# Down projection: both weight sums ahead of the first split, and one low part of 2560 columns for two pieces

## What is computed

```python
h = rms_norm(x, ffn_norm[l])
x = x + conv_ffn(h, w_ffn_up[l], ffn_conv_w[l], ffn_conv_b[l], w_ffn_down[l])

def conv_ffn(h, w_up, conv_w, conv_b, w_down):
    ...
    a, b = jnp.split(u, 2, axis=-1)
    return (jax.nn.silu(a) * b) @ w_down
```

## Time and profile before

| what | value |
|---|---|
| median of 3 runs | 1081.53 us (1081.53 to 1081.56) |
| span of the profiled execution, first to last instruction | 1079.9 us |
| TensorE busy | 1075.4 us of the span |
| VectorE busy | 909.8 us, 1374 instructions |
| ScalarE busy | 630.3 us |
| mean granted TensorE clock | 0.999 of full speed |

### The profile page before, as it was taken

How to read it: one execution, slowest core, us unless ns; L and a number is a source line. 1 busy time by engine, 2 the same in 40 slices (tenths; PEclk the granted TensorE clock), 3 DMA queues, 4 the chain that set the end, 5 groups by cost and what they waited for, 6 DMA issues and landing times.

```text
span 1079.9 us, 18178 instructions
## 1 busy us (share of the span) xinstructions
PE 1075.4 (100%) x6549; PEld 930.3 (86%) x6549; DVE 909.8 (84%) x1374; ACT 630.3 (58%) x926; POOL 70.9 (7%) x100
## 2 busy tenths in 40 slices
PE   9999999999999999999999999999999999999998
PEld 9888888888888888888888888888888888888887
DVE  7878988889655678888888888888877899999997
ACT  7677676756544655555555555545555566646663
POOL 4500000000000000000000000000000000000000
PEclk9999999999999999999999999999999999999999
DMA  8654677777787978888887878788887877887882
GB/s 273 184 157 147 201 199 237 183 243 199 229 234 257 267 212 242 228 240 212 252 226 227 244 212 255 220 238 237 252 231 223 239 250 270 284 276 254 287 313 94
DMA packets 185086, 249.08 MB, mean 231 GB/s; under 512 B 9141, under 2 KB 143174, under 8 KB 184774
## 3 DMA queue, kind: packets, MB, share of 16 engines
q1 hardware_dynamic: 170134, 212.30, 61.0%
q0 software_dynamic: 12480, 31.46, 15.1%
q10 hardware_dynamic: 2416, 4.60, 1.2%
HBM read 243.75 MB, written 36.04 MB: 259 GB/s over the span
## 4 chain that ended last, share of the span: by engine, by line
PE 99%; DMA 0%; DVE 0%; issue 0%; DVEq 0%
PE bank L1791 38%; PE bank L1799 20%; PE bank L2186 7%; PE bank L2185 7%; PE bank L2184 7%; PE bank L2037 3%; PE bank L1838 3%; PE bank L2039 3%; PE bank L1840 3%; PE bank L1839 3%; PE bank L2038 3%; PE bank L1759 1%; PE bank L1867 1%; PE bank L2076 0%; DMA xt<-in_x_dram 0%; PE bank L1956 0%
## 5 line engine op out<-in xcount | busy, mean ns | idle before, releaser
L764 ACT CAST w_hi<-raw 128x1024 fp32r<-128x1024 f32 x299 | 312.2, 1049 | 255.2 <-PE bank L1799 121.9
L1173 DVE TENSOR_TENSOR w_lo<-raw,w_hi 128x1024 fp32r<-128x1024 f32 x299 | 364.2, 1223 | 110.4 <-ACT w_hi L764 109.8
L1791 PE MATMUL bank<-hs,w_hi 128*128 128x512 f32 x1792 | 423.0, 391 | 0.0
L1791 PEld LDWEIGHTS bank<-hs,w_hi 128*128 128x128 f32 x1792 | 331.2, 188 | 66.3 <-issue 0.9
L1799 PEld LDWEIGHTS bank<-hs,w_lo 128*128 128x128 f32 x1792 | 224.5, 191 | 5.7 <-issue 0.2
L1799 PE MATMUL bank<-hs,w_lo 128*128 128x256 f32 x1792 | 227.3, 283 | 0.0
L1143 ACT CAST hi_slot<-slot 128x1024 fp32r<-128x1024 f32 (+1 forms) x96 | 111.0, 1187 | 68.1 <-DVE slot L1716 33.3
L1700 DVE TENSOR_TENSOR slot_lo<-slot,hi_slot 128x1024 fp32r<-128x1024 f32 (+1 forms) x96 | 128.7, 1387 | 4.7 <-ACT hi_slot L1143 3.7
L2186 PE MATMUL bank<-hi_slot,gated 128*128 128x512 f32 (+1 forms) x202 | 78.2, 387 | 0.0
L2184 PE MATMUL bank<-hi_slot,gated 128*128 128x512 f32 (+1 forms) x202 | 78.2, 387 | 0.0
L1618 DVE SCALAR_TENSOR_TENSOR C<-U,cols,C 128x256 f32<-128x256 f32 x176 | 73.3, 479 | 0.0
(11 more groups left out here) (247 smaller groups left out, 1176.7 us busy)
## 6 DMA issues: line engine op xcount, KB each, us to landing
raw<-in_w_ffn_up_dram SPq DMA_DIRECT2D x176, 512.0 KB, 4.8
u_sums<-in_w_ffn_down_dram POOLq DMA_DIRECT2D x60, 512.0 KB, 6.9
raw<-in_w_in_dram SPq DMA_DIRECT2D x51, 512.0 KB, 4.6
slot<-in_w_ffn_down_dram SPq DMA_DIRECT2D x36, 512.0 KB, 5.0
raw<-in_w_in_dram SPq DMA_DIRECT2D x66, 256.0 KB, 3.3
raw<-in_w_out_dram SPq DMA_DIRECT2D x32, 512.0 KB, 5.2
slot<-u_sums SPq DMA_DIRECT2D x60, 256.0 KB, 5.5
slot<-in_w_ffn_down_dram SPq DMA_DIRECT2D x30, 256.0 KB, 4.0
```

Source lines behind the costliest of these rows:

```text
L764: act.copy(w_hi[:, i, :], raw[:, i, :]).then_inc(units_hi, 1)
L1173: dve.tensor_tensor(w_lo[:, i, :], raw[:, i, :], w_hi[:, i, :].bitcast(F32), ALU.subtract)\
L1791: m = pe.matmul(banks[b][:, :], w_hi[:, i, c], hs[:, 4 * i + k, :], start=(first and k == 0), stop=(final and k == 3))
```

## The change

Only VectorE's program for S quadruples changes. Both sums now come first, then the low part of a, and then one subtraction of 2560 columns makes the low parts of b and c together. It waits for the high part of c and then counts `units_split` up by two. The diff also brings code for a third sum in DRAM, for the quadruples named in `SECOND_SUM_IN_DRAM`; that tuple is empty, so the branches that test it never act. The DRAM tensor `u_sums` gets room for three sums per quadruple instead of two, which moves the addresses of the two that are used.

```diff
+SECOND_SUM_IN_DRAM = ()
...
-        u_sums = nc.dram_tensor("u_sums", (SEVENS * 2 * P, 2 * GT), F32)
-        u_sums_v = u_sums.ap().rearrange("(n j p) (c m) -> n j p c m", j=2, p=P, m=GT)
+        u_sums = nc.dram_tensor("u_sums", (SEVENS * 3 * P, 2 * GT), F32)
+        u_sums_v = u_sums.ap().rearrange("(n j p) (c m) -> n j p c m", j=3, p=P, m=GT)
...
-                before = raw_piece_before(q, "c")
-                if before is not None:
-                    wait_until_used(dve, before)
-                elif SLOT_OF[q] == 2:
-                    wait_until_used(dve, LAST_OLD)
-                dve.tensor_tensor(t2, t1, b21, ALU.add).then_inc(t2_made, 1)
-                dve.wait_ge(t2_made, s + 1)
+                if second_sum_in_dram(q):
+                    dve.wait_ge(second_sum_loaded[SLOT_OF[q]], second_sums_loaded(q))
+                else:
+                    before = raw_piece_before(q, "c")
+                    if before is not None:
+                        wait_until_used(dve, before)
+                    elif SLOT_OF[q] == 2:
+                        wait_until_used(dve, LAST_OLD)
+                    dve.tensor_tensor(t2, t1, b21, ALU.add).then_inc(t2_made, 1)
+                    dve.wait_ge(t2_made, second_sums_made(q))
                 dve.tensor_tensor(t4, t2, b22, ALU.add).then_inc(t4_made, 1)
 
+            def split_both(q):
+
+                dve.wait_ge(units_hi, piece_number(q, "c") + 1)
+                blocks = slice(blocks_of(q, "b").start, blocks_of(q, "c").stop)
+                raw_b_and_c, lo_b_and_c = [slots[SLOT_OF[q]][as_lo][:, blocks, :] for as_lo in range(2)]
+                dve.tensor_tensor(lo_b_and_c, raw_b_and_c, hi_slots[q % HI_SLOTS][:, blocks, :].bitcast(F32),
+                                  ALU.subtract).then_inc(units_split, 2)
+
             def lo_of(pair, at):
 
                 q = q_of(pair, at)
+                if is_seven(pair, at):
+                    sums_of_weights(pair, at)
+                    split(q, "a")
+                    dve.wait_ge(t4_made, seven_of(pair, at) + 1)
+                    split_both(q)
+                    return
                 for piece in pieces_of(q):
-                    if piece == "b" and is_seven(pair, at):
-                        sums_of_weights(pair, at)
-                        dve.wait_ge(t4_made, seven_of(pair, at) + 1)
                     split(q, piece)
```

More of the change, by code:

```diff
@@ L363, in hybrid_layer @@
         down_loaded = {piece: [sem(f"down_loaded_{piece}{n}") for n in range(SLOTS)] for piece in "ab"}
+        second_sum_loaded = [sem(f"second_sum_loaded{n}") for n in range(SMALL_SLOT)]
         four_loaded = {piece: [sem(f"four_loaded_{piece}{n}") for n in range(SMALL_SLOT)] for piece in "ab"}
@@ L426, in seven_of, with second_sum_in_dram, second_sums_loaded, second_sums_made @@
             return pair * SEVENS + SEVEN_AT[pair].index(at)
+        def second_sum_in_dram(q):
+            pair, at = divmod(q, QUADRUPLES)
+            return is_seven(pair, at) and K_PAIR_AT[pair][at] in SECOND_SUM_IN_DRAM
+        def second_sums_loaded(q):
+            n = sum(second_sum_in_dram(m) and SLOT_OF[m] == SLOT_OF[q] for m in range(OLD_RING, q + 1))
+            return 16 * n
+        def second_sums_made(q):
+            return sum(is_seven(*divmod(m, QUADRUPLES)) and not second_sum_in_dram(m) for m in range(q + 1))
         def pieces_of(q):
@@ L634, in wait_for_slot @@
                 elif SLOT_OF[q] == 2:
-                    wait_until_used(sp, LAST_OLD - 3 if piece == "a" else LAST_OLD - 1)
+                    wait_until_used(sp, LAST_OLD - {"a": 3, "b": 1, "c": 0}[piece])
                 elif SLOT_OF[q] == SMALL_SLOT and piece == "b":
@@ L649, in load_seven @@
                 sp.dma_start(raw_of(q, "b")[:, 2, :], u_sums_v[n, 0, :, pair, :]).then_inc(b_loaded, 16)
+                if second_sum_in_dram(q):
+                    wait_for_slot(q, "c")
+                    sp.dma_start(raw_of(q, "c")[:, 0, :], u_sums_v[n, 2, :, pair, :])\
+                        .then_inc(second_sum_loaded[SLOT_OF[q]], 16)
             def load_four(pair, at):
@@ L662, in _ @@
             wait_until_used(sp, Q_DOWN * RING - 1)
-            sp.wait_ge(sums_added, 16 * 2 * SEVENS)
+            sp.wait_ge(sums_added, 16 * (2 * SEVENS + len(SECOND_SUM_IN_DRAM)))
             for pair in range(COLUMN_PAIRS):
@@ L738, in column_block @@
                 return w_down_v[:, tile, :].rearrange("p (pair c m) -> p pair c m", c=2, m=GT)[:, :, c, :]
+            step, copied, added = 0, 0, 0
             for n in range(SEVENS):
-                wait_for_step(4 * n)
+                wait_for_step(step)
                 pool.dma_start(u_sums_v[n, 0], column_block(2 * n, 1)).then_inc(sums_copied, 16)
-                wait_for_step(4 * n + 1)
+                wait_for_step(step + 1)
                 pool.dma_start(u_sums_v[n, 1], column_block(2 * n + 1, 0)).then_inc(sums_copied, 16)
-                wait_for_step(4 * n + 2)
-                pool.wait_ge(sums_copied, 16 * 2 * (n + 1))
+                step, copied = step + 2, copied + 2
+                if n in SECOND_SUM_IN_DRAM:
+                    wait_for_step(step)
+                    pool.dma_start(u_sums_v[n, 2], column_block(2 * n + 1, 0)).then_inc(sums_copied, 16)
+                    step, copied = step + 1, copied + 1
+                wait_for_step(step)
+                pool.wait_ge(sums_copied, 16 * copied)
                 for j in range(2):
-                    wait_for_step(4 * n + 2 + j)
+                    wait_for_step(step + j)
                     pool.dma_start(u_sums_v[n, j], column_block(2 * n, 0), accum_op=ALU.add).then_inc(sums_added, 16)
+                step, added = step + 2, added + 2
+                if n in SECOND_SUM_IN_DRAM:
+                    wait_for_step(step)
+                    pool.wait_ge(sums_added, 16 * added)
+                    pool.dma_start(u_sums_v[n, 2], u_sums_v[n, 0], accum_op=ALU.add, max_dma_last_dim=2 * GT * 4).then_inc(sums_added, 16)
+                    step, added = step + 1, added + 1
         @block.scalar
@@ L1708, in sums_of_weights @@
                 wait_for_down(dve, q, "b")
-                before = raw_piece_before(q, "c")
-                if before is not None:
-                    wait_until_used(dve, before)
-                elif SLOT_OF[q] == 2:
-                    wait_until_used(dve, LAST_OLD)
-                dve.tensor_tensor(t2, t1, b21, ALU.add).then_inc(t2_made, 1)
-                dve.wait_ge(t2_made, s + 1)
-                dve.tensor_tensor(t4, t2, b22, ALU.add).then_inc(t4_made, 1)
+                if second_sum_in_dram(q):
+                    dve.wait_ge(second_sum_loaded[SLOT_OF[q]], second_sums_loaded(q))
[7 more added lines that the diff above has]
+                    dve.wait_ge(t2_made, second_sums_made(q))
+                dve.tensor_tensor(t4, t2, b22, ALU.add).then_inc(t4_made, 1)
+            def split_both(q):
[4 more added lines that the diff above has]
+                                  ALU.subtract).then_inc(units_split, 2)
             def lo_of(pair, at):
                 q = q_of(pair, at)
+                if is_seven(pair, at):
[4 more added lines that the diff above has]
+                    return
                 for piece in pieces_of(q):
-                    if piece == "b" and is_seven(pair, at):
-                        sums_of_weights(pair, at)
-                        dve.wait_ge(t4_made, seven_of(pair, at) + 1)
                     split(q, piece)
```

## The result

| kernel | median us | lowest to highest | runs |
|---|---|---|---|
| before | 1081.53 | 1081.46 to 1081.98 | 17 |
| changed | 1083.59 | 1082.35 to 1084.55 | 17 |

The ratio on record is 1.0017, with a 95% interval of 1.0011 to 1.0024; the two medians of the table lie 2.06 us apart. The changed kernel is slower. By the ratio it is so by less than the 0.2% named in the prediction, but the interval reaches over that line. The forecast was 1082.8 and the range 1081.4 to 1084.8. What stands out beside the median is the spread: 0.5 us between the runs of the kernel before, 2.2 us between those of the changed one.

The account below looks back on a forecast made before the run. TensorE, busy for 1075.4 of 1079.9 us, was taken to bound the kernel. Delays of 0.51 + 0.63 + 0.15 = 1.3 us on 1081.53 gave 1082.8 us, with a range of 1081.4 to 1084.8.

Parts of the forecast that it names:

- TensorE sets the pace, VectorE's savings are worth nothing: In Down TensorE never waits, so the 3.0 us gained on VectorE over 30 S quadruples is worth nothing.
- Piece b becomes late, at the ends of runs: In S quadruples b is ready only when c is: 5.39 us from t1's landing, where it was 3.36.
- Quadruple 8: 0.51 us; quadruple 37: 0.63: At two ends of runs, TensorE waits for piece b behind t1's load, by 0.51 and 0.63 us.
- The period of 5.29: VectorE's time per S quadruple from sum to sum: 5.29 us after the change, 5.39 before, a saving of 0.10.
- a hop of 0.03, so the large subtraction starts at 2.54: In an S quadruple, VectorE's large subtraction starts 0.03 us after ScalarE's copy of c, 2.54 after t2 starts.
- The merge's own saving: In each S quadruple, one large subtraction for two saves VectorE 0.08 us (1.67 + 1.14 against 2.75).
- Quadruples 14, 20, 31: 0.15 us in all: Three ends of runs with 0.1 to 0.3 us to spare, given 0.15 us of delay in all.
- Quadruple 14 follows from 13, whose load lands at 917.66: Chain from that load makes 14's large subtraction end at 928.34; TensorE wants it at 928.60, 0.16 us to spare.
- r = 0.10: The hop to TensorE when piece b is ready, taken as 0.10 us, near the short hops between engines.
- Later loads, the slower rival: Piece b's loads 0.5 us longer: 3.0 us more, 1084.5; or VectorE period 5.40, every run ending in a stall; chance 0.27.
- VectorE leading: VectorE sets the matmuls' pace in Down, so 0.10 us per S quadruple comes back: 1078.5 us; chance 0.04.
- VectorE's busy time: Over the kernel, 30 merges at 0.15 us each should cut it by 4.5 us, to about 905.4.

Follow-up runs that it names:

- the order alone: Changed kernel with both sums still first, but separate low parts of b and c as before: 1081.42 us, ratio 1.0000.
- the merge alone: Changed kernel with the 2560-column low part kept, but the low part of a put back ahead of the sums: 1112.33 us, ratio 1.0284.
- one wait less: Changed kernel without VectorE's own wait for t4 ahead of the large subtraction: 1083.25 us, ratio 1.0015.

## Why the prediction was right, step by step

| quadruple | forecast, us | stall in the profile after, us |
|---|---|---|
| 8 | 0.51 | 0.34 |
| 37 | 0.63 | 0.84 |
| 14, 20 and 31 together | 0.15 | 0.45 |
| 25 | none | 0.13 |
| all | 1.3 | 1.8 |

*TensorE sets the pace, VectorE's savings are worth nothing.* Right, and shown: the order alone, and the merge everywhere but at six ends of runs, both give 1081.4 to 1081.5.

*Piece b becomes late, at the ends of runs.* Right. Splitting it again at six places takes back all of the loss. The size fits too: for each kernel tried, from the order alone to the merge alone, the time of the profiled execution less what TensorE lost in Down lies between 1081.3 and 1081.9 us, which is where the runs of the kernel before lie.

*Quadruple 8: 0.51 us; quadruple 37: 0.63.* The mechanism was right. In the profiled execution they cost 0.34 and 0.84, in that with old addresses 0.71 and 0.76, in that with one wait less 0.90 and 0.82. Their landings differ between executions by some tenths. I put the spread of 2.2 us down to this; what speaks for it is that the runs lie within 0.7 us where none of the six places stalls, but each kernel has only one trace.

*The period of 5.29.* Wrong by 0.09. The step "a hop of 0.03, so the large subtraction starts at 2.54" failed: this hop is 0.13 with two waits ahead of the large subtraction and 0.10 with one. The 0.03 is what a low part of 1024 columns showed. The rows of before had 0.10 where it mattered: at quadruple 8, start the low part of b at 895.99, and the copy before it started at 894.40 and lasts 1.49, as another of 1536 columns does. The merge's own saving came as the spacing had it, 2.74 us from the large subtraction to the next instruction; the round trip ate it. (Its size was 0.06 by the prediction's own terms, 1.67 + 1.14 - 2.75, not 0.08, and landing to low part is 5.37 by its own sum, the figure it went on with, not 5.39.)

*Quadruples 14, 20, 31: 0.15 us in all.* Mis-sized: they cost 0.14 to 0.16 each. The step "Quadruple 14 follows from 13, whose load lands at 917.66" named the wrong chain. In the trace after, that load lands at 917.4, before VectorE comes for it at 917.87; the chain starts when TensorE leaves the D. Quadruple 25 was not named at all: its run begins late behind the merge of the first column pair, whose adds hold ScalarE back for 3.9 us, and it costs 0.13.

*r = 0.10.* The hop to TensorE is 0.06, but each of the six stalls costs 0.11 more at the second matmul, a term that the sum did not have. Six times that is 0.7 us, more than the difference between the forecast of 1.3 and the 1.8 seen.

*Later loads, the slower rival.* Its place was right, and the runs at the high end (up to 1084.55) are of its kind; its price of 3.0 was not reached by the median. The rival had a second form, a VectorE period of 5.40, with which every run ends in a stall. That is nearly what came: 5.38, and a stall at six of seven ends, where the forecast spoke of two to five. (By the rival's own sum 5 x 5.38 + 2.28 = 29.2 us would just have fitted; the wait for the D, which neither had, makes up the rest.) So what happened at 14, 20 and 31 is nearer to the rival than to the forecast, and there is luck in the number: the terms that were too small (the hop, the second matmul, quadruple 25) did not add up to the 0.9 us that parted the forecast from the 0.2% line, and by the medians they came within 0.1 us of it.

*VectorE leading* is ruled out by the order alone, in whose trace the period is 5.27 us instead of 5.39 and whose time is that of before. *VectorE's busy time* fell by 1.8 us to 908.0, not by 4.5: the 30 large ones last 2.825 us as forecast, but the time in which two instructions overlap had been counted once before too. Of the signs named, there were no stalls in the middle of runs and none over 1 us; but the copy of c did not leave ScalarE's waits, which still have 14.8 us for the second sum, after 33.3.

What stays open: how the 0.35 us between the profiled execution and the median of the changed kernel divides over 8 and 37; and why t1 lands late at just these two. The loads of 14 and 31 have the same two D transfers behind them and took 5.7 and 5.5 us in the trace after, where 8 and 37 took 6.4 and 6.9.

## What to carry to other kernels

Merging two instructions on a producer that is not the bottleneck saves what nobody waits for, and delays the first half of its result until the inputs of the second half are there; read the slack of that first half at its tightest places, here the ends of runs, not in the mean. Where a step is a round trip between two engines, something independent has to lie inside it: that was worth 29 us here (1112.3 against 1083.6), far more than the merge. And a change that eats slack can show in the spread between runs: here it grew from 0.5 to 2.2 us, while the median moved by 0.2%.

## What the runs showed of the hardware

A stall of TensorE costs more than the delay of its first matmul. At all six places of the changed kernel the second matmul came 0.33 to 0.34 us after the first, not 0.227, even where the first was only 0.05 us late or less. This is no fixed floor: in the run with one wait less the first matmul of quadruples 14, 25 and 31 was on time and only the second came late, by 0.04 to 0.07 us. TensorE's granted clock stayed at 1.00 through these stalls, over the whole of 860 to 1080 us.

A semaphore wait that has already been met is not free on VectorE when it stands next to one that has not: 0.13 us from the end of ScalarE's copy to the start of the large subtraction with two waits, 0.10 with one, and 0.03 where a low part of 1024 columns carried its one wait itself. Why the large subtraction does not carry its wait, no run tells.

And a 256 KB load of t1 from DRAM took 4.7 to 8.5 us from issue in the trace after. Two 512 KB transfers right behind it in the same queue are a part of this for 8 and 37 (6.4 and 6.9 us with them, 5.7 and 5.4 without), and the same two ahead of it made it 8.0 and 8.1; but they are not the whole, since 14 and 31 had them behind too. Moved either way, these transfers made the kernel slower.
